# Feed-forward matmuls that take the high and the low input together: 512 columns for a high weight, 256 for a low one

## The reference

```python
f = jnp.square(jax.nn.relu(h @ w_ff1[l])) @ w_ff2[l]
```

## Time and profile before

| What | us |
|---|---|
| median of 3 runs | 2695.38 |
| lowest and highest run | 2691.3, 2696.39 |
| the profiled run's own time | 2687.95 |
| its span in the profile | 2686.3 |

### The profile page before, as it was taken

How to read it: one execution, slowest core, us unless ns; L and a number is a source line. 1 busy time by engine, 2 the same in 40 slices (tenths; PEclk the granted TensorE clock), 3 DMA queues, 4 the chain that set the end, 5 groups by cost and what they waited for, 6 DMA issues and landing times.

```text
span 2686.3 us, 54234 instructions
## 1 busy us (share of the span) xinstructions
PE 2595.0 (97%) x21636; PEld 2438.7 (91%) x21636; DVE 1937.1 (72%) x2030; ACT 1111.6 (41%) x1271; POOL 171.3 (6%) x281
## 2 busy tenths in 40 slices
PE   5999999999999999999998999999989999999998
PEld 2776778899999999998998999999979999999997
DVE  2475586887787776878878988888776566575664
ACT  2333443444443443434443444544444344443443
POOL 5000000111010010110000000001010000000000
PEclk8999999999999999999999999999999999999998
DMA  9997856688888887886766765568847676676763
GB/s 362 367 357 271 258 189 218 196 294 311 285 296 294 280 303 245 295 286 204 256 212 201 235 222 163 181 225 289 280 158 234 197 238 213 199 244 205 234 200 114
DMA packets 304452, 658.80 MB, mean 245 GB/s; under 512 B 31200, under 2 KB 37688, under 8 KB 303928
## 3 DMA queue, kind: packets, MB, share of 16 engines
q1 hardware_dynamic: 272056, 539.35, 59.6%
q0 software_dynamic: 32256, 117.45, 13.4%
HBM read 654.62 MB, written 2.10 MB: 244 GB/s over the span
## 4 chain that ended last, share of the span: by engine, by line
PE 82%; DVE 9%; DMA 5%; ACT 2%; issue 2%; SPq 1%; ACTq 0%; DVEq 0%; POOLq 0%
PE ps L1858 24%; PE ps L1860 24%; PE ps L1859 24%; DVE lo L1043 2%; DMA proj<-in_w_ada 2%; DMA raw<-in_w_in 2%; PE ps L1901 1%; PE ps L1903 1%; PE ps L1902 1%; ACT hi L638 1%; DMA ada_ring<-in_w_ada 1%; PE ps L2052 1%; PE ps L1843 1%; DVE work L1055 1%; DVE proj L1215 1%
## 5 line engine op out<-in xcount | busy, mean ns | idle before, releaser
L1043 DVE TENSOR_TENSOR lo<-raw,hi 128x1024 fp32r<-128x1024 f32 x868 | 1048.7, 1222 | 580.1 <-ACT hi L638 577.6
L638 ACT ACTIVATE hi<-raw 128x1024 fp32r<-128x1024 f32 x868 | 909.7, 1059 | 1216.6 <-PE ps L1860 863.9
L1858 PE MATMUL ps<-acts,hi 128*128 128x256 f32 x4432 | 1236.5, 279 | 24.0 <-DVE lo L1043 16.1
L1859 PE MATMUL ps<-acts,hi 128*128 128x256 f32 x4432 | 1224.0, 276 | 0.0
L1860 PE MATMUL ps<-acts,lo 128*128 128x256 f32 x4432 | 1223.9, 276 | 0.0
L1858 PEld LDWEIGHTS ps<-acts,hi 128*128 128x128 f32 x4432 | 854.1, 193 | 60.8 <-issue 32.4
L1859 PEld LDWEIGHTS ps<-acts,hi 128*128 128x128 f32 x4432 | 854.3, 193 | 1.6 <-issue 1.0
L1860 PEld LDWEIGHTS ps<-acts,lo 128*128 128x128 f32 x4432 | 854.2, 193 | 0.4
L1858 PE MATMUL ps<-f_acts,hi 128*128 128x256 f32 x2048 | 565.0, 276 | 2.9 <-DVE lo L1043 2.8
L1860 PE MATMUL ps<-f_acts,lo 128*128 128x256 f32 x2048 | 563.2, 275 | 0.0
L1859 PE MATMUL ps<-f_acts,hi 128*128 128x256 f32 x2048 | 563.2, 275 | 0.0
(11 more groups left out here) (267 smaller groups left out, 1376.5 us busy)
## 6 DMA issues: line engine op xcount, KB each, us to landing
raw<-in_w_ff SPq DMA_DIRECT2D x512, 512.0 KB, 4.8
raw<-in_w_in SPq DMA_DIRECT2D x232, 512.0 KB, 4.7
ada_ring<-in_w_ada POOLq DMA_DIRECT2D x224, 512.0 KB, 5.3
proj<-in_w_ada SPq DMA_DIRECT2D x92, 512.0 KB, 8.6
ada_ring<-in_w_ada SPq DMA_DIRECT2D x40, 512.0 KB, 6.4
raw<-in_w_out SPq DMA_DIRECT2D x32, 512.0 KB, 5.3
raw<-in_w_o SPq DMA_DIRECT2D x32, 512.0 KB, 5.5
work<-in_w_ada SPq DMA_DIRECT2D x28, 512.0 KB, 6.4
```

Source lines behind the costliest of these rows:

```text
L638: nc.scalar.activation(hi[n % SPLIT][:, :], raw[n % RAW][:, :], ACT.Copy).then_inc(hi_ready, 1)
L1043: V.tensor_tensor(lo[n % SPLIT][:, :], raw[n % RAW][:, :], hi[n % SPLIT][:, :].bitcast(F32), ALU.subtract)\
L1858: M(out, h, right_hi, start=start, stop=False)
L1859: M(out, h, right_lo, start=False, stop=False)
```

## The change

In 28 of the 32 groups of each feed-forward (all but the last four down groups) `wide_group` takes the place of `group`. For a k tile it first issues the four matmuls of the high weight blocks j = 0 to 3, each with 512 columns, the high and the low input together, and then the four of the low weight blocks with the 256 columns of the high input. An output tile j now fills a whole bank, one half with the sum of high-input products and the other with the low-input one, so a group takes four banks (`wide_banks`), 0 to 3 or 4 to 7 in turn. The two halves are added when they are taken out. After an up group ScalarE copies the first half into `cross`, VectorE adds the second half, and one VectorE instruction computes relu(x) times x in place. After a down group VectorE adds the halves into `y` one after the other. The four idle transposes in `quarter` are gone. Since banks 4 to 7 are now used by groups too, the sums of the background rows come one chunk later in the last quarter of ff1 and wait for the group before, and its second group waits for `mod_ready`. The rest of the change passes the new arguments on.

```diff
...
@@ -336,6 +336,12 @@
         def out_banks(g, tiles=4):
 
             return ps[:, 2 * (g % 2):2 * (g % 2) + 2, :].rearrange("p b (j n) -> p (b j) n", n=S)[:, 0:tiles, :]
+
+        def wide_banks(g):
+
+            base = "ff1" if g < first["qk2a"][1] else "ff2"
+            b = 4 * ((g - first[base][1]) % 2)
+            return ps[:, b:b + 4, :]
 
 
         OUT1 = [(4 * h + q, q, HALF * h + c) for h in range(2) for q in range(4) for c in range(HALF)]
...
@@ -646,6 +652,10 @@
                         index_relu(batches[c])
                 if kind == "up":
                     act.wait_ge(acts_ready, split_done["ffn" if up < 4 * QUARTERS else "preffn"])
+                    act.wait_ge(weights_used, n + per + d)
+
+                    act.wait_ge(group_out, g + dg)
+                    nc.scalar.activation(halves(cross[:, :, :]), natural(wide_banks(g)[:, :, 0:S]), ACT.Copy).then_inc(first_copied, 1)
                     act.wait_ge(squared, up + 1 + dup)
                     nc.scalar.activation(f_acts[:, tile, 0:S], cross[:, :, :], ACT.Copy).then_inc(ff_hi, 1)
                 if kind == "gate":
...
@@ -1111,12 +1121,20 @@
             def up(tile, k, dk):
 
                 def run(left):
-                    V.tensor_scalar(halves(cross[:, :, :]), natural(left), 0.0, None, ALU.max).then_inc(relued, 1)
-                    dve.wait_ge(relued, k + 1 + dk)
-                    V.tensor_tensor(halves(cross[:, :, :]), halves(cross[:, :, :]), natural(left), ALU.mult).then_inc(squared, 1)
+                    dve.wait_ge(first_copied, k + 1 + dk)
+                    V.tensor_tensor(halves(cross[:, :, :]), halves(cross[:, :, :]), natural(left[:, :, S:2 * S]), ALU.add).then_inc(ff_summed, 1)
+                    dve.wait_ge(ff_summed, k + 1 + dk)
+                    V.scalar_tensor_tensor(cross[:, :, :], cross[:, :, :], 0.0, cross[:, :, :], ALU.max, ALU.mult).then_inc(squared, 1)
                     dve.wait_ge(ff_hi, k + 1 + dk)
                     V.tensor_tensor(f_acts[:, tile, S:2 * S], cross[:, :, :], f_acts[:, tile, 0:S].bitcast(F32), ALU.subtract)\
                         .then_inc(group_out, 1)
+                return run
+
+            def down_wide(tile, k, dk):
+                def run(left):
+                    V.tensor_tensor(halves(y[:, tile, :]), halves(y[:, tile, :]), natural(left[:, :, 0:S]), ALU.add).then_inc(down_half, 1)
+                    dve.wait_ge(down_half, k + 1 + dk)
+                    V.tensor_tensor(halves(y[:, tile, :]), halves(y[:, tile, :]), natural(left[:, :, S:2 * S]), ALU.add).then_inc(group_out, 1)
                 return run
 
             def down(tile):
...
@@ -1858,6 +1877,28 @@
                 M(out, h, right_hi, start=start, stop=False)
                 M(out, h, right_lo, start=False, stop=False)
                 return M(out, l, right_hi, start=False, stop=stop)
+
+            def wide_group(n, g, d=0, dg=0, src=acts, fresh=None, after={}):
+
+                free(g, dg)
+                out = wide_banks(g)
+                for c in range(FULL):
+                    slot = (n + c) % SPLIT
+                    pe.wait_ge(lo_ready, n + c + 1 + d)
+                    h = hi[slot][:, :].rearrange("p (t n) -> p t n", n=NC)
+                    l = lo[slot][:, :].rearrange("p (t n) -> p t n", n=NC)
+                    for t in range(CK):
+                        k = CK * c + t
+                        if fresh and k in fresh:
+                            pe.wait_ge(*fresh[k])
+                        both = src[:, k, :].rearrange("p (w a n) -> p w n a", w=2, a=2)
+                        for j in range(4):
+                            M(out[:, j, :], h[:, t, j * P:(j + 1) * P], both, start=k == 0, stop=False)
+                        for j in range(4):
+                            last = M(out[:, j, 0:S], l[:, t, j * P:(j + 1) * P], moved(src[:, k, 0:S]), start=False, stop=k == KT - 1)
+                    last.then_inc(weights_used, 1)
+                    if c in after:
+                        after[c]()
 
             def group(n, g, per=FULL, d=0, dg=0, src=acts, tile0=0, width=NC, places=(0, 1, 2, 3), fresh=None, middle=None, batches={},
                       pairs=False, after={}):
...
@@ -2375,12 +2416,11 @@
             def quarter(n0, g0, dq, fresh=None, last=False):
                 with pe.Fori(0, 2) as i:
                     for u in range(2):
-                        group(n0 + FULL * u, g0 + u, FULL, dq * (8 * FULL) + i * (2 * FULL), dq * 8 + i * 2, fresh=fresh if u == 0 else None)
-                idle_turns()
+                        wide_group(n0 + FULL * u, g0 + u, dq * (8 * FULL) + i * (2 * FULL), dq * 8 + i * 2, fresh=fresh if u == 0 else None)
                 with pe.Fori(0, 2) as i:
                     for u in range(2):
-                        group(n0 + (4 + u) * FULL, g0 + 4 + u, FULL, dq * (8 * FULL) + i * (2 * FULL), dq * 8 + i * 2, src=f_acts,
-                              fresh={KT - 4: (group_out, dq * 8 + (g0 + 4))} if u == 0 else None)
+                        wide_group(n0 + (4 + u) * FULL, g0 + 4 + u, dq * (8 * FULL) + i * (2 * FULL), dq * 8 + i * 2, src=f_acts,
+                                   fresh={KT - 4: (group_out, dq * 8 + (g0 + 4))} if u == 0 else None)
 
             def feed_forward(phase, name, after):
                 n0, g0 = first[phase]
...
@@ -2389,12 +2429,19 @@
                 e = QUARTERS - 1
                 n0, g0 = n0 + 8 * FULL * e, g0 + 8 * e
                 if phase == "ff1":
+                    def middle_sums():
+                        pe.wait_ge(group_out, g0)
+                        for k in range(3):
+                            sum_rows(5 + k, k)
+
                     for u in range(4):
-                        group(n0 + FULL * u, g0 + u, after={} if u else {1: lambda: [sum_rows(5 + k, k) for k in range(3)], 4: lambda: turn_sums(5), 5: lambda: turn_sums(6, ready=3), 6: lambda: turn_sums(7, ready=3)})
+                        if u == 1:
+                            pe.wait_ge(mod_ready, 6)
+                        wide_group(n0 + FULL * u, g0 + u, after={} if u else {2: middle_sums, 4: lambda: turn_sums(5), 5: lambda: turn_sums(6, ready=3), 6: lambda: turn_sums(7, ready=3)})
                 else:
                     with pe.Fori(0, 2) as i:
                         for u in range(2):
-                            group(n0 + FULL * u, g0 + u, FULL, i * (2 * FULL), i * 2)
+                            wide_group(n0 + FULL * u, g0 + u, i * (2 * FULL), i * 2)
                 for q in range(4):
                     group(n0 + (4 + q) * FULL, g0 + 4 + q, src=f_acts, fresh={KT - 4: (group_out, g0 + 4)} if q == 0 else None, after=after(q))
 
...
@@ -2476,8 +2523,12 @@
             idle_products(2, 2)
             spread_root(ps[:, 5, S:2 * S])
             idle_products(1, 2)
+            def last_sum():
+                pe.wait_ge(group_out, first["ff2"][1] + 8 * QUARTERS - 4)
+                sum_rows(11, 0)
+
             feed_forward("ff2", "preffn", lambda q: {4: lambda: piece_stats("postffn", q - 1)} if q
-                         else {3: lambda: sum_rows(11, 0), 6: lambda: turn_sums(11)})
+                         else {3: last_sum, 6: lambda: turn_sums(11)})
             piece_stats("postffn", 3)
             gather_stats("postffn")
             spread_root(ps[:, 7, 0:S])
...
```

More of the change, by code:

```diff
@@ L236, in build @@
         squared, ff_hi, gate_exp, gate_plus, gated = (sem(n) for n in ("squared", "ff_hi", "gate_exp", "gate_plus", "gated"))
-        relued = sem("relued")
+        first_copied, ff_summed, down_half = (sem(n) for n in ("first_copied", "ff_summed", "down_half"))
         ada_used, acc_cleared, seg_reduced, mod_ready = (sem(n) for n in ("ada_used", "acc_cleared", "seg_reduced", "mod_ready"))
@@ L1070, in finish_row, with group @@
                                 vecs[:, b:b + KT].rearrange("p (j c) -> p j c", c=4), ALU.add).then_inc(mod_ready, 1)
-            def group(n, g, per=FULL, d=0, dg=0, tiles=4, adas=(), out=None, middle=None, batches={}, after={}, out_first=False):
-                halves = ADA * len(adas)
+            def group(n, g, per=FULL, d=0, dg=0, tiles=4, adas=(), out=None, middle=None, batches={}, after={}, out_first=False, wide=False):
+                ada_steps = ADA * len(adas)
                 for c in range(per):
@@ L1077, in group @@
                         split_chunk(n + c + SPLIT, d)
-                    for h in range(c * halves // per, (c + 1) * halves // per):
+                    for h in range(c * ada_steps // per, (c + 1) * ada_steps // per):
                         ada(h % ADA, *adas[h // ADA])
@@ L1089, in group @@
                 dve.wait_ge(weights_used, n + per + d)
-                out(out_banks(g, tiles))
+                out(wide_banks(g) if wide else out_banks(g, tiles))
                 if out_first:
@@ L1600, in up_groups, with down_groups @@
                         group(n + FULL * u, g + u, FULL, dn + i * (2 * FULL), dg + i * 2, adas=adas(i, u),
```

(13 more changed lines are left out.)

## The result

The kernel after takes 2669.2 us (median of 4 runs, 2667.85 to 2672.64), the kernel before, run beside it, 2694.6 us (median of 4, 2691.3 to 2696.39): ratio 0.9909, 95% interval 0.9892 to 0.9926. It is 25.4 us faster; 28.5 were forecast, 2667 us. The profiled run of after took 2670.27 us, its span is 2668.6.

The account below looks back on a forecast made before the run. TensorE's matmul stream was taken to bound both feed-forwards; 26.9 + 2.6 - 1 = 28.5 us off the median of 2695.38 gave 2667 us, range 2656 to 2685.

Parts of the forecast that it names:

- The stream: Both feed-forwards' matmuls: one of 512 columns replaces two of 256, 0.48 us less in each of 56 groups, 26.9 us.
- the 0.3 us that would have made the prediction wrong: Sign in the ff1 loop: a saving per group under 0.3 us would show the prediction wrong.
- rival 4: 512-column matmuls: reading two runs 256 columns apart slows the stream; at 5% the kernel takes 2706 us; chance 0.06.
- Rival 1: Low-weight matmuls go faster in the mixture, 109.1 ns each; 36.2 us from the stream, 2658 us in all; chance 0.09.
- Rival 2: Matmul stream: a matmul that goes is worth 2.4 ns, not 7.5; 10 us gained, 2685 us; chance 0.08.
- The idle transposes: Between up and down loops: four transposes cost 0.44 us, go six times, and cover nothing needed; 2.6 us gained.
- Taking groups out: End of up and down groups: the new copy, sums and second additions stay hidden, cost 0.
- rival 3: End of up groups: the new work shows, fifth chunk 0.5 us late in 32 groups, 16 us, 2683 us; chance 0.11.
- its two bounds: Upper bounds on taking groups out: 21 us for 32 up groups, 27 us for 24 down groups.
- The last quarter of ff1: Its four up groups: w_ada rows come no earlier, so half of their 1.9 us gain is lost, 1 us.
- The level: Whole kernel: 28.5 us off the runs' median of 2695.38 us, giving 2667 us.

Follow-up runs that it names:

- high_split: The kernel after with each 512-column matmul of a high weight issued as two of 256 columns, all else kept: 2688.74 us, ratio 0.9984.
- low_half: The kernel after with each low-weight matmul on 128 of its 256 columns, the rest of that product left out: 2665.66 us, ratio 0.99.
- in_turn: The kernel after with high and low weight matmuls of each output tile issued in turn, not four and then four: 2666.81 us, ratio 0.9903.
- before's second profile: The kernel before, unchanged, profiled once more: 2691.65 us.
- the eased kernels: The kernel after with, in ff1, w_ada transfers cut to 128 of 1024 columns (2657.44 us), or VectorE's instruction on its rows to 64 of 1024 (2656.43 us).

## Why the prediction was right, point by point

**The stream (26.9 us): right where it could be seen alone.** In ff2 the width brings 13.2 us, by after against high_split, where 28 x 0.48 = 13.4 was the term. In ff1 it brings 8.85 for the same term, for the reasons under the last quarter below. Over the six looped pieces of ff1 that is 8.7 us for 24 groups, 0.36 us a group, and 0.42 with the transposes, against before: above the 0.3 us that would have made the prediction wrong. Steps, seams and period are those forecast, and the walk over two runs 256 columns apart (rival 4) costs nothing: 0.86 us for four. Rival 1 fell with the 0.45 us for four low matmuls, and low_half says that even half the columns would not have made a k tile shorter. Rival 2 fell too: a matmul that goes is worth 13.2 us / (28 x 64), 7.4 ns, in ff2. Why two of 256 columns cost more than one of 512 I left open. A matmul of 256 with its own block costs 111.7 ns, 5.0 more than its columns at 2.4 GHz, and one of 512 costs 215.8, only 2.5 ns more than its (I wrote 2.4); that the 111.7 ns are the block's load is likely and not shown. The 109.2 ns that the Trainium skill (TensorE: Matmul & The Clock Gate, Back-to-back issue gap) gives for 256 columns aren't reached by any stream with a block for each matmul here. That section calls its formula the gap of a single matmul and says that in a stream of loads and matmuls both set the spacing; the prediction applied it to a stream without saying so.

**The idle transposes (2.6 us): right.** 1.31 us for three in ff2. In ff1 they are 0.36 us in the first piece and 0.08 and 0.36 in turn in the others, by before against high_split, so 1.3 us as well.

**Taking groups out (0): right in ff2, not quite in ff1.** The new relu-and-square took 1.22 us, not 1.28. The slack in ff1 is small, as I wrote, and a few times it was used up. The longest of these in the loops, ScalarE of after:

```profile
753.17 1.07 ACT L644 ACTIVATE hi<-raw 128x1024 fp32r<-128x1024 f32 x1 [3.30 <-DMA raw<-in_w_ff]
...
755.78 1.06 ACT L644 ACTIVATE hi<-raw 128x1024 fp32r<-128x1024 f32 x1 [1.54 <-DMA raw<-in_w_ff]
756.75 1.01 ACT L658 ACTIVATE cross<-ps 128x1024 f32<-128x1024 f32 x1
...
761.82 1.06 ACT L660 ACTIVATE f_acts<-cross 128x1024 f32 x1 [4.07 <-DVE cross L1127]
```

VectorE of after, against the earlier trace rows:

```profile
758.01 1.28 DVE L1065 SCALAR_TENSOR_TENSOR work<-ada_ring,silu,work 128x1024 f32 x1
759.21 1.21 DVE L1125 TENSOR_TENSOR cross<-cross,ps 128x1024 f32<-128x1024 f32 x1
760.46 1.22 DVE L1127 SCALAR_TENSOR_TENSOR cross<-cross 128x1024 f32<-128x1024 f32 x1
763.14 1.23 DVE L1129 TENSOR_TENSOR f_acts<-cross,f_acts 128x1024 f32 x1 [1.45 <-ACT f_acts L660]
764.28 2.35 DVE L1053 TENSOR_TENSOR lo<-raw,hi 128x1024 fp32r<-128x1024 f32 x2
```

And TensorE of after:

```profile
763.55 0.61 PE L1898 MATMUL ps<-acts,lo 128*128 128x256 f32 x4
765.55 1.13 PE L1896 MATMUL ps<-acts,hi 128*128 128x512 f32 x4 [1.40 <-DVE lo L1053]
```

Two weights landed late, so the last split before the copy began at 755.78, VectorE came to the sum only at 759.21, and the `lo` that TensorE needed began at 764.28. The piece took 85.50 us where 83.84 are usual: 1.7 us. That is rival 3, and it is not the only place. In ff1 TensorE waits for `lo` at the fifth chunk behind an up group four times in after, for 0.33, 1.40, 1.06 and 1.62 us, 4.4 us in all, and twice in before, for 1.3 us. So this term was about 3 us in ff1 and not 0 (the last two of the four waits lie in the last quarter, told of next), and nothing in ff2; rival 3 had asked for over 10 us. Of its two bounds I wrote that they would end just above the range: 21 us would give 2688, but 27 us 2694, which is no gain at all.

**The last quarter of ff1 (-1 us): the term that was mis-sized.** The change had 14.8 us to bring in ff1 (28 x 0.48 + 1.3), I took 1 off, and 9.5 to 10.0 came. 1.7 us are the hole above (in_turn has one like it at another place, so it is not tied to a group). Most of the rest is in the last quarter (pieces 7 and 8). Its up groups are 1.6 us shorter than in before, its down groups, whose code is the same, 1.6 us longer (2.2 by before's second profile), so that nothing of the 1.9 us was left: the quarter takes 183.3 us before and after. About 0.6 us more is in the first piece (87.24 where the eased kernels have 86.6) and 0.3 in small waits of the others. VectorE of after, at the end of the last up groups and in a down group, waits for a row each time:

```profile
1114.66 1.29 DVE L1065 SCALAR_TENSOR_TENSOR work<-ada_ring,silu,work 128x1024 f32<-128x1024 f32 x1 [2.31 <-DMA ada_ring<-in_w_ada]
...
1141.84 1.28 DVE L1065 SCALAR_TENSOR_TENSOR work<-ada_ring,silu,work 128x1024 f32<-128x1024 f32 x1 [4.37 <-DMA ada_ring<-in_w_ada]
```

TensorE of after behind them, at the fifth chunk of the first down group and the second chunk of the second one:

```profile
1129.81 0.38 PE L1877 MATMUL ps<-f_acts,hi 128*128 128x256 f32 x1 [1.62 <-DVE lo L1053]
...
1144.31 0.38 PE L1877 MATMUL ps<-f_acts,hi 128*128 128x256 f32 x1 [0.84 <-DVE lo L1053]
```

Being sooner in the four up groups bought nothing, most likely because the ring gives its rows no sooner: the time saved is waited for in the down groups behind. I let half of 1.9 us go. By the two kernels with the ring eased after loses 5.8 us and more in this quarter (183.3 against 177.4 and 176.1). My reading of the earlier trace rows stopped at TensorE's 3.6 us of waits and didn't ask which stream behind it had a pace of its own.

**The level (2667):** 25.4 us between medians against 28.5 forecast; by stages 9.5 to 10.0 and 14.5, some 24 us. What lies between 24 and 25.4 is inside what the middle moves from run to run.

## What to carry to other kernels

Take the cost of a matmul from the period of the stream that it is in, and with a new weight block for each, look for a floor under it: here 111.7 ns, at 256 columns as at 128, likely the block's load. When a stream gets faster, look for everything beside it that has its own pace (here a ring of two whose next transfer waits for the last one's use), and ask whether it sets the stage where it sits before you credit that stage with the stream's gain: the last quarter of ff1 gained nothing. Judge a change of 1% by the stages that it touches, when other stages move by 6 us between two profiles.

## What the runs showed that I had not expected

Halving the columns of every low matmul leaves ff2 at 680.90 us to the hundredth, and so does putting the matmuls in another order. Neither transfers nor VectorE make ff1's holes alone: easing either one by itself took 8.4 and 9.7 us off ff1. And the last quarter of ff1 takes 183.3 us with 512-column matmuls in its up groups and 183.4 without.
